# One-core decoder layer: first down chunks ahead of the first gathers, 80-row lists for the middle ranks, split casts in the light stage

## The reference, cut to what matters

```python
def hier_moe(x, wg, bg, we, be, w1, w3, w2):
    ...
    expert = g_idx * EXPERTS_PER_GROUP + e_idx        # two of 32 for each token
    ...
    hdn = jax.nn.silu(xb @ w1[e]) * (xb @ w3[e])      # 1024 -> 512, twice
    return hdn @ w2[e]                                # 512 -> 1024
    ...
    out = zeros.at[row_tok].add(y * row_w[:, None])
```

## Time and profile before

| what | value |
|---|---|
| median of three runs | 1173.18 us |
| the profiled execution's own time | 1172.78 us |
| its span, first to last instruction | 1171.0 us |
| PE busy (matmuls) | 1115.4 us, 95% |
| DVE busy | 879.3 us, 75% |
| ACT busy | 695.1 us, 59% |
| POOL busy | 338.9 us, 29% |
| mean granted TensorE clock | 0.984 |

### The profile page before, as it was taken

The page is one execution under the profiler, slowest core; times in us unless marked ns, Lnnn a source line. Parts: engine busy times, 40 slices in busy tenths (PEclk is TensorE's granted clock), DMA queues, the critical chain, the costliest instruction groups (busy, mean ns, idle before and its releaser), DMA issues.

```text
span 1171.0 us, 17312 instructions
## 1 busy us (share of the span) xinstructions
PE 1115.4 (95%) x5838; PEld 860.2 (73%) x5839; DVE 879.3 (75%) x1298; ACT 695.1 (59%) x958; POOL 338.9 (29%) x394
## 2 busy tenths in 40 slices
PE   6999999999999989999699999999999999999997
PEld 5877887767777678888567777777777777777775
DVE  4424323666566788888679999999999999999995
ACT  5425202544455544434347777777777788888884
POOL 1211102321111221222463242323424245444211
PEclk9998999999999999999789999999999999999999
DMA  8130302110200263342589999999999999999992
GB/s 323 47 108 1 108 1 72 35 65 28 99 28 18 91 186 140 131 177 95 206 319 385 373 393 380 380 395 372 392 377 378 389 376 385 398 391 385 395 390 66
DMA packets 66912, 271.66 MB, mean 232 GB/s; under 512 B 12757, under 2 KB 19481, under 8 KB 42393
## 3 DMA queue, kind: packets, MB, share of 16 engines
q1 hardware_dynamic: 57000, 245.32, 53.8%
q0 software_dynamic: 6384, 19.14, 7.1%
q10 hardware_dynamic: 3456, 6.29, 1.4%
HBM read 246.74 MB, written 26.48 MB: 233 GB/s over the span
## 4 chain that ended last, share of the span: by engine, by line
PE 80%; DVE 10%; ACT 5%; issue 2%; POOL 2%; DMA 1%; ACTq 0%; POOLq 0%; SPq 0%; DVEq 0%
PE main_pm L693 13%; PE main_score L693 7%; PE main_score L2084 5%; PE main_score L2086 5%; PE main_score L2085 5%; DVE main_w_low L2054 4%; PE main_score L754 3%; PE main_pt L2086 3%; PE main_pt L2084 3%; PE main_po L2086 3%; PE main_po L2084 3%; PE main_pt L2085 3%; PE main_po L2085 3%; ACT main_w_high L2050 2%; PE main_pt L2096 2%
## 5 line engine op out<-in xcount | busy, mean ns | idle before, releaser
L2054 DVE TENSOR_TENSOR main_w_low<-w_raw,main_w_high 128x2048 fp32r<-128x2048 f32 x190 | 434.0, 2291 | 38.8 <-ACT main_w_high L2050 36.9
L2050 ACT CAST main_w_high<-w_raw 128x2048 fp32r<-128x2048 f32 x190 | 362.5, 1909 | 68.5 <-PE main_score L2086 52.2
L1953 POOL DMA_INDIRECT main_xg<-xn_dram,main_token x32 | 79.0, 2468 | 275.4 <-DVE main_token L1926 264.5
L2084 PE MATMUL main_score<-main_w_high,main_hT_high 128*96 128x512 f32 x256 | 102.6, 401 | 1.1 <-DVE main_hT_low L2345 0.6
L2086 PE MATMUL main_score<-main_w_high,main_hT_low 128*96 128x512 f32 x256 | 100.7, 393 | 0.0
L2085 PE MATMUL main_score<-main_w_low,main_hT_high 128*96 128x512 f32 x256 | 100.3, 392 | 0.0
L693 PE MATMUL main_pm<-slot_high,xh 128*128 128x512 f32 x208 | 87.7, 422 | 2.1 <-DVE slot_low L1404 2.1
L693 PE MATMUL main_pm<-slot_low,xh 128*128 128x512 f32 x208 | 82.9, 398 | 0.0
L693 PE MATMUL main_pm<-slot_high,xl 128*128 128x512 f32 x208 | 82.8, 398 | 0.0
L1998 POOL DMA_INDIRECT out<-main_y,main_dest x31 | 50.0, 1614 | 89.3 <-ACT main_y L2010 60.7
L1055 ACT ACTIVATE main_prob<-main_score,main_nmax 128x128 f32<-128x128 f32 (+7 forms) x64 | 47.6, 744 | 33.4 <-DVE main_nmax L1463 32.5
(11 more groups left out here) (375 smaller groups left out, 2615.9 us busy)
## 6 DMA issues: line engine op xcount, KB each, us to landing
w_raw<-in_moe_w SPq DMA_DIRECT2D x192, 1024.0 KB, 19.6
slot_raw<-in_w_in SPq DMA_DIRECT2D x12, 1024.0 KB, 7.3
main_x<-in_x SPq DMA_DIRECT2D x8, 512.0 KB, 11.2
slot_raw<-in_w_out SPq DMA_DIRECT2D x4, 1024.0 KB, 6.8
main_hx<-in_x SPq DMA_DIRECT2D x8, 512.0 KB, 3.9
out<-main_hx SPq DMA_DIRECT2D x8, 512.0 KB, 2.6
xn_dram<-main_xn SPq DMA_DIRECT2D x8, 512.0 KB, 2.8
gr_dram<-main_stage ACTq DMA_DIRECT2D x8, 256.0 KB, 2.0
```

What stands on the lines that cost most here:

```text
L1953: nc.gpsimd.indirect_dma_start(xg[u][0:slots], None, s["xn2_dram"], bass.IndirectOffsetOnAxis(token[u][0:slots, 0:1], 0), bounds_check=bou ...
L2050: nc.scalar.copy(wh[slot(c, e)][:], raw[u][c // 2][:, c % 2, :]).then_inc(w_high, 1)
L2054: nc.vector.tensor_tensor(wl[slot(c, e)][:], raw[u][c // 2][:, c % 2, :], wh[slot(c, e)][:].bitcast(F32), ALU.subtract).then_inc(w_low, 1)
L2084: nc.tensor.matmul(out, x_hi, w_hi, start=start, stop=False)
```

## The change

- Heavy ranks change places. Ranks 0 to 2 stay at places 0 to 2, ranks 6 to 17 go to places 3 to 14 (`MIDDLE`), ranks 3 to 5 to places 15 to 17, and the light ones stay. A table `rank_at` is filled by POOL with four iotas in the front (at the step where `xg[0]` is cleared), and `seats` compares with it. `seats` makes the offset in three DVE ops where there was one.
- Places 3 to 14 scatter 80 rows in place of 96 (`slots_of`). Their one-hots, gathers, transposes and matmuls keep 96.
- For light experts chunk 0 is cast by ACT in two halves of 1024 columns with a semaphore after each, and DVE subtracts in two halves, the first as soon as the first cast half is there.
- `dve_targets` of e+2 moves from behind low of chunk 4 to the end of DVE's work for e, behind low of chunk 1 of e+1, for all experts from 1 on, heavy and light.
- SP issues chunks 2 and 3 of expert 1 ahead of its wait for the first gathers; 4 and 5 stay behind it.
- The two output gains count on the semaphore of the other small loads (`head_in`, 160 in all) in place of their own.

```diff
@@ -48,8 +48,10 @@
 NEG = -1e30
 BUCKETS, MAX_DIST = 32, 128
 CAP = 96
+MIDDLE_CAP = 80
 LIGHT_CAP = 64
 HEAVY = 18
+LARGEST, MIDDLE = 6, range(3, 15)
 MORE = -(-SEQ // CAP) - 1
 REL = 3 * P
 CW = 256
...
@@ -522,8 +525,13 @@
 
         V = nc.vector
         dve.wait_ge(order_step, RANKED)
-        V.tensor_tensor(seat[:], iota_e[0:NE, :], acc[1][0:NE, 0:NE], ALU.is_equal).then_inc(order_step, 1)
-        V.tensor_scalar(s["offset"][:], acc[0][:, 0:NE], HEAVY - 0.5, float(CAP - LIGHT_CAP), ALU.is_gt, ALU.mult)
+        dve.wait_ge(flagged, T)
+        V.tensor_tensor(seat[:], rank_at[0:NE, :], acc[1][0:NE, 0:NE], ALU.is_equal).then_inc(order_step, 1)
+        V.tensor_scalar(middle_offset[:], acc[0][:, 0:NE], LARGEST - 0.5, float(CAP - MIDDLE_CAP), ALU.is_gt,
+                        ALU.mult)
+        dve_then(dve, V.tensor_scalar(s["offset"][:], acc[0][:, 0:NE], HEAVY - 0.5, float(MIDDLE_CAP - LIGHT_CAP),
+                                      ALU.is_gt, ALU.mult))
+        dve_then(dve, V.tensor_tensor(s["offset"][:], s["offset"][:], middle_offset[:], ALU.add))
 
     def number_mm(pe):
 
...
@@ -1367,6 +1375,10 @@
             if n == T - 1:
                 pool.wait_ge(g_o_mm, T)
                 clear_rows(0)
+                for to, first_rank in ((slice(0, MIDDLE.start), 0), (slice(MIDDLE.start, MIDDLE.stop), LARGEST),
+                                       (slice(MIDDLE.stop, HEAVY), MIDDLE.start), (slice(HEAVY, NE), HEAVY)):
+                    pool_then(pool, nc.gpsimd.iota(rank_at[:, to], pattern=[[1, to.stop - to.start]], base=first_rank,
+                                                   channel_multiplier=0, allow_small_or_imprecise_dtypes=True))
             if n < T:
                 g_root(n)
                 if n >= 2:
...
@@ -2054,14 +2067,25 @@
         nc.vector.tensor_tensor(wl[slot(c, e)][:], raw[u][c // 2][:, c % 2, :], wh[slot(c, e)][:].bitcast(F32),
                                 ALU.subtract).then_inc(w_low, 1)
 
-    def low_half(dve, e, u, c, half):
-        if half == 0:
-            dve.wait_ge(w_high, number(e, c) + 1)
-        w = slice(half * D, half * D + D)
-        done = nc.vector.tensor_tensor(wl[slot(c, e)][:, w], raw[u][c // 2][:, c % 2, w],
-                                       wh[slot(c, e)][:, w].bitcast(F32), ALU.subtract)
-        if half == 1:
-            done.then_inc(w_low, 1)
+    def high_by_half(act, e, r, u):
+
+        act.wait_ge(raw_in[u][0], 16 * (r + 1))
+        act.wait_ge(chunk_used, number(e, 0) - 2)
+        for half in range(2):
+            w = slice(half * D, half * D + D)
+            nc.scalar.copy(wh[slot(0)][:, w], raw[u][0][:, 0, w]).then_inc((w_half, w_high)[half], 1)
+
+    def low_by_half(dve, e, u):
+
+        for half in range(2):
+            if half == 0:
+                dve.wait_ge(w_half, e - HEAVY)
+            else:
+                dve.wait_ge(w_high, number(e, 0) + 1)
+            w = slice(half * D, half * D + D)
+            done = nc.vector.tensor_tensor(wl[slot(0)][:, w], raw[u][0][:, 0, w], wh[slot(0)][:, w].bitcast(F32),
+                                           ALU.subtract)
+        done.then_inc(w_low, 1)
 
     def sp_expert(sp, e, r, j, last, light, tail=False):
         if not some(e, 2):
@@ -2293,7 +2317,9 @@
             more = (0, 1) if not (last and j == 3) else ()
         else:
             more = ()
-        if more:
+        if more and light[1]:
+            high_by_half(act, e + 1, pair(r, j, 1), 1 - u)
+        elif more:
             high(act, e + 1, pair(r, j, 1), 1 - u, 0)
         if last and j == 3:
             high(act, e + 1, pair(r, j, 1), 1 - u, 2)
@@ -2377,8 +2403,6 @@
             dve_x(dve, 1, 1)
             dve_ids(dve, 2, 1, 2)
             dve_targets(dve, 2, 1, 2)
-        elif not (last and j >= 2):
-            dve_targets(dve, e + 2, r + 1, (j + 2) % 4)
         if some(e, 1) and not (last and j == 3):
             dve_x(dve, e + 1, 1 - u, light[2])
         if not (last and j >= 1):
@@ -2386,7 +2410,10 @@
         if some(e, 1):
             low(dve, e, u, 5)
         if not (last and j == 3):
-            low(dve, e + 1, 1 - u, 0)
+            if light[1]:
+                low_by_half(dve, e + 1, 1 - u)
+            else:
+                low(dve, e + 1, 1 - u, 0)
         if not last:
             dve.wait_ge(listed_rows, e + 3)
             pick(q, e + 4, e + 4, u, place_of[u][:], LIGHT_CAP if light[5] else CAP)
@@ -2394,6 +2421,8 @@
             low(dve, e + 1, 1 - u, 1)
         else:
             low(dve, e + 1, 1 - u, 2)
+        if some(e, 1) and not (last and j >= 2):
+            dve_targets(dve, e + 2, r + 1, (j + 2) % 4)
 
     def list_token(dve, e):
 
@@ -2445,7 +2474,12 @@
                 for half in range(2):
                     scatter_half(pool, e - 1, 1 - u, (j - 1) % 4, half)
             else:
-                scatter(pool, q, q, e - 1, 1 - u, (j - 1) % 4, slots=LIGHT_CAP if light[0] else CAP)
+                scatter(pool, q, q, e - 1, 1 - u, (j - 1) % 4, slots=slots_of(e - 1, light[0]))
+
+    def slots_of(e, light):
+
+        middle = e in MIDDLE if isinstance(e, int) else not light
+        return LIGHT_CAP if light else MIDDLE_CAP if middle else CAP
 
     def pair(r, j, d):
 
@@ -2469,9 +2503,11 @@
         expert(eng, NE, NE // 2, 0, True, [True, False, False], tail=True)
 
     def sync(sp):
+        for chunk in (2, 3):
+            load_chunk(sp, a, s, 1, 1, chunk, 1, 0)
         for u in range(2):
             sp.wait_ge(q.xg_in[u], 16)
-        for chunk in (2, 3, 4, 5):
+        for chunk in (4, 5):
             load_chunk(sp, a, s, 1, 1, chunk, 1, 0)
         over_experts(sp, sp_expert)
 
```

More of the change, by code:

```diff
@@ L352, in stage_front @@
     rel_in, bias_in, z_in = sem("rel_in"), sem("bias_in"), sem("z_in")
-    gain_in, head_in = sem("gain_in"), sem("head_in")
+    head_in = sem("head_in")
     rel_out, filled, rel_step, lam_step = sem("rel_out"), sem("filled"), sem("rel_step"), sem("lam_step")
@@ L1431, in lam_part @@
             if stage_ == 0:
-                dve.wait_ge(head_in, 128)
+                dve.wait_ge(head_in, 160)
                 for i in range(2):
@@ L2020, in stage_experts @@
     listed_rows = sem("rows_of_list_ready")
+    w_half = sem("w_high_half_ready")
     slT_ready, hT_ready = sem("silu_turned_ready"), sem("hidden_turned_ready")
```

7 lines of the change are left out of this document (4 added, 3 removed).

## The result

| | before | after |
|---|---|---|
| median of 13 runs each | 1171.98 us | 1175.46 us |
| lowest, highest | 1169.63, 1173.31 | 1173.65, 1178.69 |
| profiled execution, its span | 1172.78, 1171.0 | 1174.89, 1173.1 |

The ratio of the times is 1.0038, with a 95% interval of 1.0028 to 1.0047: the changed kernel is slower by 3.3 to 5.5 us. The prediction said 1172.4, a gain of 0.4 us. The time lies inside its range of 1167.0 to 1178.2, above the forecast and under the 1176.7 from which it would have said slower (0.18); the sum had the wrong sign all the same.

A forecast was written before the change was run, and what follows sets the result against it. It took PE to bound the heavy stage and a PE-ACT-DVE chain the light one. Pair +2.2, halves -2.9 and early loads +0.3 made -0.4 on 1172.78: 1172.4 us, range 1167.0 to 1178.2.

The forecast's parts named there:

- The pair, heavy stage: Moved `dve_targets` delays `main_hd` by 0.20, 0.11 of it paid in 13 experts: +2.2 us, ends 0 and 3.4.
- The halves: Light stage, 13 hand-overs: halved chunk 0 casts cut the period from 16.90 to 16.70: -2.9 us, ends 0 and -6.0.
- the pair itself is neutral in this loop, which holds it in either spot: Light loop through the cast and low of chunk 0: moving `dve_targets` was to cost nothing there.
- the second rival: Pair delays `main_hd` by 3.4 in all and pushes `main_hT_low` past its 0.50 spare, light gain 0: 1178.2 us, chance 0.18.
- In it only DVE's idle can go: Light loop of two experts, 33.80 us: only DVE's idle 0.57 can go, halves add 0.16, giving 33.39.
- the lower end of 16.44: Light period if only DVE's own load bounds it, halves' cost included: 13 x 0.46, or -6.0 us.
- The early loads: Start of the stage: two chunks issued before the first gather slow it slightly: +0.3 us, ends 0 and +6.0.
- mostly done when the gather's rows are read: Start of the stage: 2 MB start some 6 us ahead of the gather and need 5.5 us at 384 GB/s.
- The lists: Twelve 80-row scatters save 4.1 us of DMA time but only add to the load stream's spare: worth nothing.
- Iotas, `seats`, gains: Front edits priced at nothing, hidden by idle time; without that cover 1.1 for iotas, 0.20 for `seats`.
- The first (DVE's load): Halves give all they can, light period falls to DVE's load, heavy stage pays nothing: 1167.1 us, chance 0.20.
- The third, DMA as the bound: Load stream sets the end, so 4.1 us of scatters and 5.5 of early loads come off: 1163.2 us, chance 0.07.

The follow-up runs named there:

- the pair by stage: Changed kernel with late loads, `dve_targets` in its old spot for heavy experts and between pick and low of chunk 1 for light ones: 1169.50 us, ratio 0.9982 to before.
- `dve_x` late: Before plus the halved casts, with light experts' two `dve_x` operations moved between low of chunk 5 and the first half: 1174.07 us, ratio 1.0019 to before.
- after with late loads: Changed kernel with all four chunks of expert 1 loaded behind the wait for the first gathers, as before: 1174.30 us, ratio 1.0022 to before.
- the last experiment: The pair by stage with light experts' output copies on ACT moved behind the next expert's chunk 2 cast: 1165.10 us; also with 96-row scatters and old places: 1168.16.
- halves alone: Before plus only light experts' chunk 0 casts and subtractions in halves and the gains' semaphore: 1190.59 us, ratio 1.0132 to before.
- the best version: The pair by stage with light experts' ACT output copies behind the next expert's chunk 2 cast, 80-row scatters kept: 1165.10 us, ratio 0.9945 to before.

## Why the prediction was off, step by step

The sum had -0.4 us. The table of stretches has +2.1, and the medians +3.5. Of the 2.5 between sum and table, 2.1 is the light stage, 0.6 the heavy one and 0.7 the end; the start and the last transposes give back 0.9.

- **The pair, heavy stage: right in kind, 0.6 short.** The step that took 0.11 for the 13 experts used 0.20 for the pair and 0.09 for the spare. Measured at expert 8: 0.24 and 0.08, so 0.16. `main_hd` was followed by its weight load after 0.05 in all 18, as the prediction had read it. Of its ends 0 and 3.4 it was nearer to the upper one.
- **The halves: right in size, and taken away again by the pair. This is the largest miss.** The term was -2.9, after shows -0.8, and the pair by stage -2.8 with a period of 16.72 against the 16.70 forecast. A half took 1050 ns on ACT and 1220 on DVE (1026 and 1222 forecast). The step that failed is "the pair itself is neutral in this loop, which holds it in either spot". It is neutral for the loop that was followed, through low of chunk 0. It isn't for the one that becomes the last, through `main_hT_low`, where it now stands ahead: with the pair ahead of low of chunk 1, where DVE waits anyway, the light total fell by 2.0 us (218.09 to 216.12). The prediction had this as the lower end of the term and in the second rival, with its point of decision (a spare of 0.50), and said that the two delays together "just do" exceed it, but did not let that into the sum. At a decision that close, half of the gain would have been the better term.
- **The chain's next member was put at DVE too soon.** "In it only DVE's idle can go" held, but the lower end of 16.44 was named DVE's own load without a way to get there. The period does come to 16.45 with the output copies out of ACT's part of the ring, but the agreement is in part luck: 0.3 of it is the cast that takes longer beside POOL, which the estimate did not have.
- **The early loads: the forecast of +0.3 was too low.** The gather took 5.31 us (581.15 to 586.46) where 4.3 to 5 were forecast, +0.9 over before, so "mostly done when the gather's rows are read" failed; it rested on one division of bytes by rate. In the profiled run that is won back (-0.35 at the first hidden transposes). The ratios still say 1.4 to 1.9, a good part of it in runs at a lower clock, and why is not shown. No step of the prediction looked at the clock in this stretch.
- **The end: +0.7, not in the sum.** After the last light gate the head start is waited off: PE waits 1.1 us for `main_hT_low` (the longest of its row). The kernels with the halves show 32.2 to 32.4 there (31.7 with `dve_x` late), until the outputs move (31.5, and 32.0 with 96 rows).
- **The lists: right for this kernel, for the reason given.** They are spare for the load stream. Landing late in the light stage went from 24.7 us to 15.8 (17 forecast), of which the early loads have a part: it is 18.3 in after with late loads. The spare became worth 1 to 3 us only in the faster loop of the last experiment, where that interval is wide.
- **Iotas, `seats`, gains: nothing seen**, as forecast: after with late loads needs no further term (its stretches are +2.8, -0.8 and +0.5 at the end, and its median is 2.5 over before). The four iotas took 0.80 us, and POOL's idle time ahead of `g_root` fell from 2.74 to 1.87.
- **What wasn't seen at all is what the pair is for.** No step asked who else needs DVE's pauses. The 0.48 us that the halves were to use up were POOL's time to get at SBUF, and the scatter behind the gather is waited for by the pair. Taken singly, the part that forecast a gain costs some 15 us.
- **The rivals.** The second (pair wins, slower) named the mechanism and gave 1178.2; the time fell between it and the forecast. The first (DVE's load) is the period that the last experiment reaches. The third, DMA as the bound, has no wait in after.

## What to carry to other kernels

When a wait is to be removed, list every loop that passes close to it with its spare, and let a step that stands in two of them be charged to the one that becomes the last; a spare that "just" doesn't do is a term, not a bound. Before DVE's idle time is filled, ask what POOL does in it: indirect DMAs issued by POOL, and those queued behind them, can depend on that pause. Then look in the new trace whether the gathers got longer, since here some kernels without a pause let them in and some did not. Parts of a change that do nothing or harm alone can be what carries another, so undo one at a time.

## What the runs showed of the hardware that was not expected

- POOL's indirect gather is 2.4 us in before, where DVE pauses, and 5.1 to 9.6 in halves alone, where two-operand SBUF subtractions kept it out. There it gets in at idle time and at an operation that reads PSUM, and ends 0.86 us later.
- It can also get in between two subtractions with no idle time: in after and in the best version at every hand-over to the first half, where the cast had ended 0.41 us before. It was kept out there at 0.58 or more, but elsewhere also at 0.40 and 0.20, so these runs give no threshold.
- The other way round, a DVE cast within SBUF took 0.58 to 0.61 us in place of 0.29 in many periods in which POOL was at work beside it.
- A stall of PE of 4.9 us was followed by a granted clock of 0.66 and 0.65 in the stretches from 985 to 995 us, and 1.00 from 995 on.
